# A causal mask and three row-to-column turns, moved from the tensor engine to the vector engine

## The reference, cut to what matters

```python
def rmsnorm(x, g):                      # one root per token
    y = xf * lax.rsqrt(jnp.mean(xf * xf, axis=-1, keepdims=True) + EPS)

def one_block(args):                    # differential attention, 128 queries, 4 heads, 2 components
    q_blk, i = args
    sc = jnp.einsum("bhcqd,bhckd->bhcqk", q_blk, k).astype(jnp.float32) * scale
    mask = kpos[None, :] <= qpos[:, None]
    sc = jnp.where(mask, sc, -jnp.inf)
    p = jax.nn.softmax(sc, axis=-1)
    a = p[:, :, 0] - lam * p[:, :, 1]
    return jnp.einsum("bhqk,bhkv->bhqv", a.astype(v.dtype), v)
```

## Time and profile before

| | |
|---|---|
| time, median of 3 runs | 2302.03 us (2301.68 to 2302.09) |
| profiled execution, first to last instruction | 2299.9 us |
| what lies around it (median less span) | 2.1 us |
| TensorE busy | 2275.5 us, 99% |
| VectorE busy | 1272.2 us, 55% |
| ScalarE busy | 654.6 us, 28% |
| GpSimd busy | 1570.5 us, 68% |
| granted TensorE clock | 0.999 of full speed |

### The profile page before, as it was taken

One profiled execution on the slowest core, in us unless ns is written; L12 is line 12 of the kernel. 1 busy time (PEld: TensorE's weight loads), 2 busy tenths in 40 slices (PEclk: granted clock), 3 DMA queues, 4 the chain that ended last, 5 costly groups with the idle time before them and its releaser, 6 DMA issues.

```text
span 2299.9 us, 27958 instructions
## 1 busy us (share of the span) xinstructions
PE 2275.5 (99%) x10600; PEld 1863.7 (81%) x10600; DVE 1272.2 (55%) x1828; ACT 654.6 (28%) x1213; POOL 1570.5 (68%) x1532
## 2 busy tenths in 40 slices
PE   8999999999999999999999999999999999999998
PEld 6888888888887788888788888888668788888887
DVE  7774745335345777166545364459875345626354
ACT  3443432101013455154311011142344233202113
POOL 8666568777776455545597777678327938878784
PEclk9999999999999999999999999999999999999999
DMA  4222232333332111212243333333113413333332
GB/s 169 82 74 86 70 92 92 105 96 97 96 97 92 51 39 49 74 34 60 73 129 100 97 114 101 93 97 105 56 37 92 124 56 92 96 98 96 99 94 76
DMA packets 112727, 200.17 MB, mean 87 GB/s; under 512 B 12497, under 2 KB 21201, under 8 KB 112593
## 3 DMA queue, kind: packets, MB, share of 16 engines
q1 hardware_dynamic: 109424, 194.72, 27.2%
q10 hardware_dynamic: 3168, 3.67, 0.5%
HBM read 196.24 MB, written 2.10 MB: 86 GB/s over the span
## 4 chain that ended last, share of the span: by engine, by line
PE 93%; DVE 4%; POOL 1%; ACT 1%; issue 0%; DMA 0%; SPq 0%; DVEq 0%; POOLq 0%; ACTq 0%
PE bank L479 27%; PE bank L481 27%; PE bank L480 27%; DVE bank L1996 1%; DVE h L1988 1%; PE bank L949 1%; PE bank L1075 1%; PE bank L528 1%; POOL wL L2857 1%; PE bank L918 1%; PE bank L919 1%; PE bank L920 1%; PE bank L598 1%; DVE aL L1996 1%; PE bank L663 1%; PE bank L926 1%
## 5 line engine op out<-in xcount | busy, mean ns | idle before, releaser
L2857 POOL TENSOR_TENSOR wL<-raw,wH 128x512 fp32r<-128x512 f32 (+2 forms) x732 | 1006.2, 1375 | 61.1
L2855 POOL TENSOR_SCALAR wH<-raw 128x512 fp32r<-128x512 f32 (+2 forms) x732 | 528.6, 722 | 553.5 <-PE bank L481 477.9
L479 PE MATMUL bank<-aH,wH 128*128 128x512 f32 (+2 forms) x1392 | 548.1, 394 | 8.6 <-DVE aL L1996 7.6
L481 PE MATMUL bank<-aH,wL 128*128 128x512 f32 (+2 forms) x1392 | 539.7, 388 | 0.0
L480 PE MATMUL bank<-aL,wH 128*128 128x512 f32 (+2 forms) x1392 | 539.6, 388 | 0.0
L479 PE MATMUL bank<-uH,wH 128*128 128x512 f32 (+1 forms) x1010 | 384.1, 380 | 0.0
L480 PE MATMUL bank<-uL,wH 128*128 128x512 f32 (+1 forms) x1010 | 382.4, 379 | 0.0
L481 PE MATMUL bank<-uH,wL 128*128 128x512 f32 (+1 forms) x1010 | 382.4, 379 | 0.0
L479 PEld LDWEIGHTS bank<-aH,wH 128*128 128x128 f32 (+1 forms) x1392 | 261.8, 188 | 64.7 <-POOL wL L2857 6.6
L480 PEld LDWEIGHTS bank<-aL,wH 128*128 128x128 f32 (+1 forms) x1392 | 261.8, 188 | 55.5 <-issue 3.2
L481 PEld LDWEIGHTS bank<-aH,wL 128*128 128x128 f32 (+1 forms) x1392 | 261.7, 188 | 54.3
(11 more groups left out here) (330 smaller groups left out, 3194.1 us busy)
## 6 DMA issues: line engine op xcount, KB each, us to landing
raw<-in_ws SPq DMA_DIRECT2D x698, 256.0 KB, 2.5
raw<-in_ws SPq DMA_DIRECT2D x24, 192.0 KB, 2.3
h<-in_xT SPq DMA_DIRECT2D x8, 256.0 KB, 6.0
E<-in_memT ACTq DMA_DIRECT2D x16, 128.0 KB, 2.6
raw<-in_ws SPq DMA_DIRECT2D x10, 128.0 KB, 2.1
tmp<-in_pT ACTq DMA_DIRECT2D x4, 256.0 KB, 2.9
out<-c_F SPq DMA_DIRECT2D x2, 512.0 KB, 2.9
out<-c_F SPq DMA_DIRECT2D x2, 384.0 KB, 2.9
```

The costliest lines, as they stand in the source:

```text
L479: P.e.matmul(o, lH, rH, start=start, stop=False, skip_group_check=skip)
L481: return P.e.matmul(o, lL, rH, start=False, stop=stop, skip_group_check=skip)
L2855: G.e.tensor_scalar(H, x, 1.0, 0.0, MUL, ADD).then_inc(*G.did("wH", n))
L2857: G.e.tensor_tensor(L, x, H.bitcast(F32), SUB).then_inc(*G.did("w", n))
```

## The change

VectorE gets an instruction that adds two tiles, scales the sum and keeps a running extreme (`tensor_tensor_reduce`). With it the mask is added where the maximum is found: `x = -(x + mask)`, in place in the bank, and the minimum of it is the negated row maximum. ScalarE then takes the exponential of -x plus that. TensorE's two mask matmuls per query tile go (line 1060), with the two ScalarE copies that made their operands. The mask tile has three tiles of zeros ahead of it, written by a `memset` over constants that are no longer used by then, for which two constants change places. The columns of the root are made by the same kind of instruction: the root's row times the identity, summed along the free axis, into a spare tile (128x256, halves in turn).

```diff
@@ consts
-CONSTS = [("ident", 128), ("ones", 128), ("perm_m", 128), ("perm_d", 128), ("dup", 128), ("dup_sw", 128),
+CONSTS = [("ident", 128), ("ones", 128), ("perm_d", 128), ("perm_m", 128), ("dup", 128), ("dup_sw", 128),
@@ build
-        d_idR, d_negR = uH[:, 3, 0:128], uH[:, 3, 128:256]
+        d_mask = cs[:, COFF["perm_m"]:COFF["perm_m"] + 512]
@@ pe
-            def columns(*sid):
-
-                b = take("col", *sid)
-                P.wait_ge(A, "rstd", *sid)
-                P.wait_ge(cs_in)
-                for n in range(4):
-                    j = P.e.matmul(b.ap[:, n:n + 1], rs[0:1, 128 * n:128 * n + 128], ones[0:1, 0:1], start=True, stop=True)
-                j.then_inc(*P.did("col", *sid))
-                give(b, V, "col", *sid)
...
-            columns("a1")
...
-            columns("n", 1)
@@ pe, d_scores
-                            P.e.matmul(bs[cmp].ap[:, 0:w], x[r, c], y[r, 0:w], start=start, stop=False, skip_group_check=True)
-                    P.wait_ge(A, "neg")
+                            j = P.e.matmul(bs[cmp].ap[:, 0:w], x[r, c], y[r, 0:w], start=start, stop=x is qL, skip_group_check=True)
+                            if x is qL:
+                                j.then_inc(*P.did("ds", hd, n, cmp))
                     for cmp in range(2):
-                        P.e.matmul(bs[cmp].ap[:, c], d_idR, d_negR, start=False, stop=True,
-                                   skip_group_check=True).then_inc(*P.did("ds", hd, n, cmp))
...
-            columns("z")
@@ act
-            do(d_idR, ident, ACT.Copy)
-            do(d_negR, cc("neg"), ACT.Copy).then_inc(*A.did("neg"))
...
-                        do(x if cmp else d_P[:, P_AT[n]:P_AT[n] + w], x, ACT.Exp, bias=sx[:, cmp:cmp + 1],
+                        do(x if cmp else d_P[:, P_AT[n]:P_AT[n] + w], x, ACT.Exp, bias=sx[:, cmp:cmp + 1], scale=-1.0,
@@ dve
-            def column(dst, *sid):
-                V.wait_ge(P, "col", *sid)
-                V.e.tensor_copy(dst, bk("col", *sid)[:, 0:4]).then_inc(*V.did("col", *sid))
+            def column(dst, spare, *sid):
+
+                V.wait_ge(A, "rstd", *sid)
+                V.wait_ge(cs_in)
+                for n in range(4):
+                    if n > 1:
+                        V.wait_ge(V, "col part", sid, n - 2)
+                    V.e.tensor_tensor_reduce(spare[:, cols128(n % 2)], rs[:, cols128(n)], ident, 1.0, 0.0, MUL, ADD,
+                                             dst[:, n:n + 1]).then_inc(*V.did("col part", sid, n))
+                V.also("col", *sid)
...
-            column(g_rc[:, :], "a1")
+            column(g_rc, g_As[:, 0:256], "a1")
...
+            V.e.memset(d_mask[:, 0:384], 0.0).then_inc(*V.did("zero"))
...
-            column(d_rc[:, :], "n", 1)
+            column(d_rc, d_P[:, 1024:1280], "n", 1)
@@ dve, d_scores
-                        V.e.tensor_reduce(sx[:, cmp:cmp + 1], bk("ds", hd, n, cmp)[:, 0:w], AX, ALU.max, negate=True).then_inc(
+                        V.wait_ge(V, "zero")
+                        x = bk("ds", hd, n, cmp)[:, 0:w]
+                        V.e.tensor_tensor_reduce(x, x, d_mask[:, 384 - 128 * n:512], -1.0, 3e38, ADD, ALU.min, sx[:, cmp:cmp + 1]).then_inc(
                             *V.did("dmax", hd, n, cmp))
...
-            column(x_rc[:, 0, :], "z")
+            column(x_rc[:, 0, :], x_P[:, 0, 0, :], "z")
```

More of the change, by code:

```diff
@@ L274 @@
     tensor_tensor = tensor_scalar = scalar_tensor_tensor = tensor_copy = tensor_reduce = op
-    tensor_tensor_scan = copy_predicated = reciprocal = memset = op
+    tensor_tensor_scan = copy_predicated = reciprocal = memset = tensor_tensor_reduce = op
 class Bank:
```

## The result

| | before | after |
|---|---|---|
| time, median of 20 runs each, same chip | 2301.38 us | 2297.69 us |
| ratio | | 0.9983, 95% interval 0.9977 to 0.999 |
| profiled span | 2299.9 us | 2296.5 us |

The account below looks back on a forecast made before the run. TensorE bounds the kernel, busy 2275.5 of 2299.9 us. Gains of 1.07 ("a1"), 2.0 (heads) and 1.07 ("z"), say 4.2 us, give 2297.8 us; likeliest range 2296 to 2299.5, wider 2294.8 to 2301.3.

Parts of the forecast that it names:

- ScalarE's diagonals: First head, before the second batch of taps: late VectorE delays them, TensorE newly waits about 1.4 us.
- tile 0's mask pair: Second head, query tile 0: removing it only lengthens TensorE's 0.60 us wait for a bank VectorE frees; no gain.
- forecast 0.5 lost against its start: Fourth head: VectorE's longer chain starts the transposes 0.5 us later relative to "mu"; all four mask pairs' gain is lost.
- The rival that everything arrives: Whole kernel: no wait replaces the removed TensorE work, all 8.0 us are gained, 2294.0 us; chance 12%.
- the columns stand behind GpSimd four times: Columns: GpSimd's lock blocks all four instructions, 6.4 us; only 0.7 us gained, 2301.3 us; chance 16%.
- the column that costs: Column "n": four VectorE instructions take 2.3 us, including about 0.8 us blocked by GpSimd.
- The tap behind them: VectorE's convolution tap after column "n", formerly at 1602.10, starts 1.54 us later, at 1603.64.
- 0.95 us later: Fourth head, "mu" to first `x_kL`: fused operations add 0.68 less 0.25 (tiles 0, 1), plus 0.25 each (tiles 2, 3).
- the 0.44 us of slack: Fourth head, first `x_kL` to first transpose: 0.51 us of slack less 0.07 for the semaphore.
- A column: At "a1", "n" and "z": TensorE loses eight tiny matmuls, 1.07 us each place, 3.2 us in all.
- A mask pair ahead of a full-height matmul: Query tiles 1 to 3: removing the pair saves TensorE 0.28 us each, read from its start to the next.
- the slower rival: Fused mask operation at three times the reduce, about 2313 us; at twice, some 1.5 us still gained; chance 5%.

Follow-up runs that it names:

- e3: The changed kernel with only the column "n" back on TensorE (tiny products and a copy): 2297.84 us.
- e4: The changed kernel with ScalarE making the second batch's four diagonals before the copy of the second channel tile's sums: 2296.25 us.
- e5: e4 with the fourth head's key tiles taken out earlier, low parts inside `combine`, ScalarE's high parts behind the exponentials: 2294.79 us.
- e1: The kernel before with only the three columns made by VectorE, the mask staying on TensorE: 2298.92 us.
- e9: The kernel before with the two new orders of e4 and e5 (diagonals first, key tiles earlier): 2301.95 us.
- e2: The changed kernel with all three columns back on TensorE, only the mask on VectorE: 2299.84 us.
- e6: The changed kernel with each fused mask operation done twice, same result: 2309.32 us.

## Why the prediction was right

**Mechanism.** Each wait stood where the prediction put it. First head: forecast 1.4 us for ScalarE's diagonals, measured 1.38, and e3 and e4 show its whole chain. Second head: tile 0's mask pair gained nothing, the wait for `uL` growing from 0.60 to 0.97. Fourth head: forecast 0.5 lost against its start, measured 0.37, by the bank of the key tile (e5); what made VectorE late there is only in part what the forecast counted, see below. The rival that everything arrives is out by these waits. That the columns stand behind GpSimd four times is out as well: of the four at "n" two were held, and the column that costs was 2.13 us for 2.3 forecast. (At "a1" three were held, 2.75 us in all, but there VectorE had time.) The tap behind them was 1.38 late (1603.00 for 1602.10, and 0.48 for what everything is earlier there), for 1.54 forecast.

**What was luck in the fourth head.** The forecast made VectorE 0.95 us later there, all of it by the fused operations. From "mu" to the first `x_kL` it does take 0.79 us more (21.35 for 20.56), but only 0.21 of that lies where fused operations stand: 0.07 at tiles 0 and 1, at tile 2 and at tile 3 each. The other 0.58 lies in three operations on two SBUF tiles each, ahead of the maxima of tile 2. Before:

```profile
1726.79 0.69 DVE L1988 TENSOR_TENSOR sq<-sq,tmp 128x512 f32<-128x512 f32 x1 [0.61 <-ACT tmp L1334]
1727.83 1.34 DVE L1988 TENSOR_TENSOR C<-C,Sn 128x512 f32<-128x512 f32 x1 [0.35 <-ACT Sn L1334]
1729.21 0.98 DVE L1988 TENSOR_TENSOR sq<-sq,C 128x512 f32<-128x512 f32 x1
```

and in the changed kernel:

```profile
1724.16 1.27 DVE L1971 TENSOR_TENSOR sq<-sq,tmp 128x512 f32<-128x512 f32 x1 [0.61 <-ACT tmp L1319]
1725.35 1.09 DVE L1971 TENSOR_TENSOR C<-C,Sn 128x512 f32<-128x512 f32 x1
1726.48 1.67 DVE L1971 TENSOR_TENSOR sq<-sq,C 128x512 f32<-128x512 f32 x1
```

The next operation starts at 1730.12 and at 1728.07, so the three take 3.33 us before and 3.91 now. GpSimd works on its pieces beside them. Before, the first of the three runs free and two are held; now the first falls into a GpSimd subtraction that ends at 1724.88, and all three are held. GpSimd starts these pieces on a release by TensorE, which without the mask pairs comes 0.75 us earlier against "mu" (6.35 us behind it for 7.10). The three take 3.33 us in e1 and e9 too, which have the old mask, and 3.9 or more in every kernel with the fused one; that GpSimd's new phase does it is argued from the rows, not tried. Without the 0.58 the fused operations would have stayed within the 0.44 us of slack, and this head would have gained some 0.2 us in place of losing 0.37 (an estimate from these numbers). The wait stood where it was forecast and near its size, but for the larger part by a hold that the forecast of this head doesn't have.

**Sizes that were off, and cancelled.**
- A column: 1.20 us for 1.07. I read the gap from start to start around the tiny products and stopped there. The first spacing behind them, 57.21 to 57.55, is 0.34 too where two matmuls are else 0.23 apart, and that went with them. Before, and then the changed kernel at the same place:

```profile
57.55 0.40 PE L480 MATMUL bank<-aL,wH 128*128 128x512 f32 x1
```

```profile
56.74 0.39 PE L478 MATMUL bank<-aH,wH 128*128 128x512 f32 x1
56.97 0.39 PE L479 MATMUL bank<-aL,wH 128*128 128x512 f32 x1
```

- A mask pair ahead of a full-height matmul gave 0.22 for 0.28, and that of tile 0, where scores follow, 0.51 for 0.37 (e2's first head: 0.51 + 3 x 0.22 = 1.17). At tile 2 the scores now border on the full-height matmul themselves, whose first spacing is 0.34 where it had been 0.29 behind the mask pair. What a removed instruction gives is its gap and the change of both neighbours' spacing.
- The fused operation: +0.03 us at 512 columns for +0.07, and the read-out near nothing of the engine's time for +0.1.
- Behind "z": +0.18 us, not forecast. It comes with every kernel that has the column "z" on VectorE (0.17 to 0.26) and is missing in e2 and e9. VectorE's `F<-F,x_stat` took 1.19 to 1.32 us three times near 1830, 0.35 to 0.69 before; TensorE's transposes behind it wait for the last of them. Each of the three hands over 0.06 to 0.08 us behind the end of a GpSimd `wL`; that the new phase against GpSimd does this is argued from the rows, not tried.

"a1", "z" and behind "z" together gave 0.1 us more than forecast, the masks of the second and third head 0.4 less, the first and fourth head 0.25 more, the stretch to "n" 0.12 less: 3.96 for 4.2.

That the time itself came within 0.1 us of the forecast (2297.69 for 2297.8) is luck as well. The forecast took 4.2 us off the first median of 2302.03; over 20 runs the kernel before has 2301.38, and 3.7 us came off that. Nor does the median stand 2.13 us above the span, as the forecast has it: in each run with both on record the time is 1.8 to 1.9 us above that run's own span. The 2.13 was the median of three runs less the span of another one.

**What was wrong.** The working of the slower rival. It let the fused operation cost twice a reduce with 1.5 us still gained, and put the turning point a little above. e6 did that and ended 7.8 us slower than before. The failed step is "VectorE's 4.6 us still fit" into 5.4 us of idle time; only some 3.2 of it was cover, and the fourth head had none. The 5% for this rival rested on a threshold that was too high; that the fused operation costs only 0.03 us more is what kept it from happening. The rival of the four blocked columns has a slip in its sum: 6.4 us from 1601.34 on put the tap 5.6 us late, as 2.3 put it 1.5 late, not 5.0; by its own further steps next to nothing would have been gained, about 2301.9 in place of 2301.3.

## What to carry to other kernels

Work taken off the bounding engine is gained only up to the next wait on the stretch; put a ledger by place beside the sum, and look at what the receiving engine's delay holds up by its order alone: two moved lines gave 1.4 us here, and nothing before the change. Count the idle time of the receiving engine as cover only where what it waits for doesn't come later by its own delay. Look, too, at the engine that the bounding one releases: GpSimd came 0.75 us earlier here and fell on other operations of VectorE. Read a removed instruction's worth from the start before it to the second start behind it.

## What the runs showed of the hardware

- Before the fused operation was timed, a half rate with two SBUF sources was considered. At 128 columns the column instructions, with two, follow each other at 0.21 us, the mask operations, with one and a bank, at 0.21 and 0.25: the half rate doesn't show. Nor does it in `F<-F,vs,C`, a scalar-tensor-tensor on two SBUF tiles: with GpSimd idle (from 1737.87 in the changed kernel) four of 512 columns took 2.74 us together and 0.75 in a row of one, as `F<-bank,d_stat,F` does.
- A read-out of 76 or 142 ns and the instruction behind it start at the same time: in the changed kernel 1731.46 for both.

```profile
1730.86 0.69 DVE L2594 CUSTOM_DVE_ANT_0 bank<-bank,cs 128x512 f32<-128x512 f32 x1
1731.46 0.14 DVE L2594 DVE_READ_ACCUMULATOR2_ANT d_stat<- 128x1 f32 x1
1731.46 0.73 DVE L2594 CUSTOM_DVE_ANT_0 bank<-bank,cs 128x512 f32<-128x512 f32 x1
```

- GpSimd's `wH<-raw`, which reads one SBUF tile, held up VectorE's column instruction just as the subtraction with two did (0.48 us at "n", 0.69 at "a1", in place of 0.28).
- A VectorE operation with a single SBUF tile can be held too: `F<-F,x_stat`, a tensor_scalar of 256 columns, took 1.19 to 1.32 us beside GpSimd in place of 0.35 near 1830 us.
- 5.1 us without a matmul brought the granted clock from 1.00 to 0.50 for over 4 us; 1.7 us did not.
